# Reading the input without its token factor for the first seven projection blocks of a fused decoder layer

## The reference

```
xn   = h * rsqrt(mean(h*h over channels) + 1e-6) * norm1        # RMSNorm: one factor per token, one per channel
proj = xn @ w_in                                                # q k v z b a c u b(sc) gate_a gate_b
qkv  = silu(causal depthwise conv of 4 taps (q, k, v))          # q, k are L2-normalised per head
beta = sigmoid(b_raw);  g = -exp(a_log) * softplus(a_raw + dt_bias)
o    = chunked gated delta rule(q, k, v, g, beta)               # 8 heads of 128
y_a  = (rms_norm(o) * silu(z)) @ w_dn_out
y_b  = (sc_b * causal depthwise conv of 3 taps (sc_c * sc_u)) @ w_sc_out
h    = h + (sigmoid(gate_a) * y_a + sigmoid(gate_b) * y_b) @ w_o
h    = h + SwiGLU FFN(rms_norm(h));  out = rms_norm(h) without the meta tokens
```

## Time and profile before

| | |
|---|---|
| time, median of 3 runs | 1100.43 us (1100.04 to 1100.97) |
| time of the profiled execution | 1099.78 us |
| its span, first to last instruction | 1097.8 us |
| mean granted TensorE clock | 0.997 |
| busy: PE | 1077.6 us, 98% of the span |
| busy: PEld, DVE, ACT, POOL | 915.6, 339.0, 467.8, 551.3 us |

### The profile page before, as it was taken

One profiled execution on the slowest core, in us unless ns is written; L12 is line 12 of the kernel. 1 busy time (PEld: TensorE's weight loads), 2 busy tenths in 40 slices (PEclk: granted clock), 3 DMA queues, 4 the chain that ended last, 5 costly groups with the idle time before them and its releaser, 6 DMA issues.

```text
span 1097.8 us, 20326 instructions
## 1 busy us (share of the span) xinstructions
PE 1077.6 (98%) x8301; PEld 915.6 (83%) x8301; DVE 339.0 (31%) x595; ACT 467.8 (43%) x1027; POOL 551.3 (50%) x479
## 2 busy tenths in 40 slices
PE   6999999999999999999999999999999999999996
PEld 6999999999999898978788888878888888888884
DVE  6344545454554545351100112222111111200002
ACT  5565656564746564743422233443222233322221
POOL 4363545444453545363544555655555555555551
PEclk9999999999999999999999999999999999999998
DMA  4222212222212122122522322222232223232322
GB/s 180 75 83 69 78 59 70 78 68 76 72 60 87 60 68 79 59 66 71 173 95 80 112 78 96 96 96 96 96 96 87 92 91 96 97 96 96 96 77 77
DMA packets 27788, 95.45 MB, mean 87 GB/s; under 512 B 2984, under 2 KB 3240, under 8 KB 27696
## 3 DMA queue, kind: packets, MB, share of 16 engines
q1 hardware_dynamic: 26496, 91.77, 25.3%
q10 hardware_dynamic: 1200, 2.38, 0.6%
HBM read 92.03 MB, written 2.11 MB: 86 GB/s over the span
## 4 chain that ended last, share of the span: by engine, by line
PE 95%; DVE 2%; issue 1%; POOL 1%; ACT 0%; DMA 0%; DVEq 0%; SPq 0%; POOLq 0%
PE bank L910 94%; DVE qkv L668 0%; DVE h L905 0%; PE bank L981 0%; POOL w_lo L292 0%; DMA h_in<-h_t 0%; DVE qkv L660 0%; DVE cv L668 0%; PE bank L1098 0%; DVE x_lo L672 0%; POOL x_lo L298 0%; PE bank L977 0%; PE bank L976 0%; ACT cbuf L397 0%; DVE h L902 0%
## 5 line engine op out<-in xcount | busy, mean ns | idle before, releaser
L292 POOL TENSOR_TENSOR w_lo<-w_raw,w_hi 128x512 fp32r<-128x512 f32 x324 | 426.1, 1333 | 489.4 <-ACT w_hi L373 489.3
L910 PE MATMUL bank<-x_hi,w_hi 128*128 128x258 f32 (+2 forms) x896 | 248.2, 335 | 5.5 <-DVE x_lo L672 4.5
L373 ACT ACTIVATE w_hi<-w_raw 128x512 fp32r<-128x512 f32 x324 | 190.1, 623 | 107.1 <-PE bank L910 106.7
L910 PE MATMUL bank<-x_hi,w_lo 128*128 128x258 f32 (+2 forms) x896 | 230.6, 316 | 0.0
L910 PE MATMUL bank<-x_lo,w_hi 128*128 128x258 f32 (+2 forms) x896 | 230.1, 315 | 0.0
L910 PE MATMUL bank<-og_hi,w_hi 128*128 128x512 f32 x416 | 164.7, 396 | 0.0
L910 PEld LDWEIGHTS bank<-x_hi,w_hi 128*128 128x128 f32 x896 | 147.0, 189 | 21.0 <-issue 4.3
L910 PE MATMUL bank<-og_hi,w_lo 128*128 128x512 f32 x416 | 164.3, 395 | 0.0
L910 PE MATMUL bank<-og_lo,w_hi 128*128 128x512 f32 x416 | 164.3, 395 | 0.0
L910 PEld LDWEIGHTS bank<-x_hi,w_lo 128*128 128x128 f32 x896 | 147.0, 188 | 11.2
L910 PEld LDWEIGHTS bank<-x_lo,w_hi 128*128 128x128 f32 x896 | 147.5, 189 | 8.6
(11 more groups left out here) (240 smaller groups left out, 1276.6 us busy)
## 6 DMA issues: line engine op xcount, KB each, us to landing
w_raw<-w_stream SPq DMA_DIRECT2D x162, 512.0 KB, 3.3
h_in<-h_t SPq DMA_DIRECT2D x4, 528.0 KB, 5.0
h<-h_t ACTq DMA_DIRECT2D x1, 2048.0 KB, 9.8
out<-h SPq DMA_DIRECT2D x8, 256.0 KB, 2.1
h_in<-gc_dram SPq DMA_DIRECT2D x7, 264.0 KB, 3.2
cst<-consts SPq DMA_DIRECT2D x1, 512.0 KB, 8.0
h_in<-gc_dram ACTq DMA_DIRECT2D x1, 264.0 KB, 3.0
sm<-small SPq DMA_DIRECT2D x1, 80.5 KB, 6.1
```

The costliest lines, as they stand in the source:

```text
L292: nc.gpsimd.tensor_tensor(w_lo[:, n % 2, at], w_raw[:, n % 3, at], w_hi[:, n % 2, at].bitcast(f32), ALU.subtract).then_inc(wlo_ready, 1)
L373: return nc.scalar.activation(to, x, ACT.Copy)
L910: return nc.tensor.matmul(o, w, x, start=start, stop=stop)
```

## The change

The input of head 0's seven blocks is the input times `norm1` alone (`xp_hi`, `xp_lo`), without the token factor; DVE multiplies each of their results by `rs1` as it leaves PSUM. The normalised input `x_hi`, `x_lo` is made in blocks 2 to 6, written in place into `h_in` first, two tiles per block, and is first read by block 7 (`PLAIN`). The token sums move from before block 0 into block 1, behind k = 2. `WARM` goes from 28 + 9 to 16. The high part of weight block 0 moves from ACT to DVE, that of block 1 ahead of ACT's loop. The `small` array (norm1 and others) is loaded first, weight block 0 right behind the first two tiles. The turn of the token projections moves from block 1 to block 2, and ACT's part of `token_factors` to quarter 3 of block 2. Up to block 7, ACT's Silu of q, k, v moves from quarter 0 to quarter 3. `rs1`, the rows of decays and a few other buffers get memory of their own, and `h_in` is protected until its low parts are made.

```diff
-WARM = 28
+WARM = 16
+PLAIN = 7
+XN_AT = {2: (0, 1), 3: (2, 3), 4: (4, 5), 5: (6, 7)}
...
 # SP
+            sp.dma_start(sm[:, :], small[:, :]).then_inc(small_in, 16)
             for part in range(4):
                 sp.dma_start(h_in[:, 2 * part:2 * part + 2, :], h_t[:, 2 * part:2 * part + 2, :]).then_inc(h_loaded[part], 16)
-            sp.dma_start(sm[:, :], small[:, :]).then_inc(small_in, 16)
-            for n in range(STREAM):
+                if part == 0:
+                    sp.dma_start(w_raw[:, 0, :], w_stream[0, :, :]).then_inc(w_in[0], 16)
+            for n in range(1, STREAM):
...
 # POOL
-            for k in range(1, KT, 2):
-                pool.wait_ge(xhi_ready, k + 1)
-                nc.gpsimd.tensor_tensor(x_lo[:, k, :], xnf[k % 4], x_hi[:, k, :].bitcast(f32),
-                                        ALU.subtract).then_inc(xlo_ready, 1)
...
             for n in range(STREAM + 1):
+                for k in XN_AT.get(n - 1, ()):
+                    pool.wait_ge(xhi_ready, k + 1)
+                    nc.gpsimd.tensor_tensor(x_lo[:, k, :], h_in[:, k, :], x_hi[:, k, :].bitcast(f32),
+                                            ALU.subtract).then_inc(xlo_ready, 1)
                 for q in range(4):
...
 # ACT
+            def plain_high(k):
                 act.wait_ge(h_loaded[k // 2], 16)
+                nc.scalar.activation(xp_hi[:, k, :], h_in[:, k, :], ACT.Copy,
+                                     scale=sm[:, NORM1 + k:NORM1 + k + 1]).then_inc(xphi_ready, 1)
+            def square(k):
                 if k >= 4:
                     act.wait_ge(x_added, max(1, k - 4))
-                nc.scalar.activation(xnf[k % 4], h_in[:, k, :], ACT.Square).then_inc(x_squared, 1)
+                nc.scalar.activation(squares[k % 4], h_in[:, k, :], ACT.Square).then_inc(x_squared, 1)
+            act.wait_ge(small_in, 16)
+            plain_high(0)
+            plain_high(1)
+            square(0)
+            square(1)
+            for k in range(2, KT):
+                plain_high(k)
...
-            split_weights(0, 0)
-            split_weights(0, 1)
+            split_weights(1, 0)
+            split_weights(1, 1)
+            for k in range(2, KT):
+                square(k)
+            act.wait_ge(ba_in, 16)
+            copy(wba_hl[:, :, 0:16], wba[:, :].rearrange("p (k c) -> p k c", c=16)).then_inc(wba_hi_ready, 1)
             act.wait_ge(x_sums, 1)
...
-            for k in range(KT):
-                act.wait_ge(xn_ready, k + 1)
-                copy(x_hi[:, k, :], xnf[k % 4]).then_inc(xhi_ready, 1)
...
                         if h < 0 and step == 22:
+                            act.wait_ge(xlo_ready, 1)
                             act.wait_ge(rows_out, 16)
...
-                if kind in ("q", "k", "v"):
+                if kind in ("q", "k", "v") and m:
...
-                if kind == "c":
+                if kind == "c" and m:
...
+                    if m == 0:
+                        act.wait_ge(z_scaled, 1)
+                    nc.scalar.activation(zs[:, m % 2, :], p[0][:, :] if m else zs[:, 0, :], ACT.Silu).then_inc(zs_ready, 1)
...
-                    if q == 0 and 2 <= n and n - 2 < MAIN and BLOCKS[n - 2][0] in ("q", "k", "v"):
+                    if q == 0:
+                        for k in XN_AT.get(n - 1, ()):
+                            act.wait_ge(xn_ready, k + 1)
+                            copy(x_hi[:, k, :], h_in[:, k, :]).then_inc(xhi_ready, 1)
+                    if q == 3 and n == 2:
+                        token_factors()
+                    if q == (0 if n > PLAIN else 3) and 2 <= n and n - 2 < MAIN and BLOCKS[n - 2][0] in ("q", "k", "v"):
                         silu(*BLOCKS[n - 2])
                     if q == 2 and n in EXP_LN_FROM:
                         nc.scalar.preload_act_table_set("natural_log_exp_and_others")
-                if n == 1:
-                    token_factors()
...
 # DVE
+            dve.wait_ge(w_in[0], 16)
+            for half in range(2):
+                at = slice(512 * half, 512 * half + 512)
+                nc.vector.tensor_copy(w_hi[:, 0, at], w_raw[:, 0, at]).then_inc(whi_first, 1)
+            dve.wait_ge(small_in, 16)
+            def plain_low(k):
+                dve.wait_ge(xphi_ready, k + 1)
+                nc.vector.scalar_tensor_tensor(xp_lo[:, k, :], h_in[:, k, :], sm[:, NORM1 + k:NORM1 + k + 1],
+                                               xp_hi[:, k, :].bitcast(f32), ALU.mult, ALU.subtract).then_inc(xplo_ready, 1)
...
+            for k in range(4):
+                plain_low(k)
+            add_square(1)
+            for k in range(4, KT):
+                plain_low(k)
+            for k in range(2, KT):
+                add_square(k)
             link(nc.vector.tensor_scalar(on_scaled[:, :], sm[:, ONORM:ONORM + 1], float(128) ** 0.5, None, ALU.mult))
-            dve.wait_ge(rs1_ready, 1)
...
             dve.wait_ge(wba_hi_ready, 1)
             nc.vector.tensor_tensor(wba_hl[:, :, 16:32], ...).then_inc(wba_ready, 1)
+            dve.wait_ge(rs1_ready, 1)
...
+                    if m == 0:
+                        dve.wait_ge(zeroed, 1)
+                        if kind == "v":
+                            dve.wait_ge(qkv_ready, 1)
+                        dve.wait_ge(rs1_ready, 1)
+                        last = CQKV + 4 * 8 * i + 3
+                        for s, part in enumerate(token_halves(kind)):
+                            ins = mult(raw[:, c % 2, 3 + part.start:3 + part.stop], p[s][:, 0:part.stop - part.start], rs1[:, part])
+                        for s, part in enumerate(token_halves(kind)):
+                            skip = META - TAIL if kind == "q" and s == 0 else 0
+                            at = slice(part.start + skip, part.stop)
+                            ins = nc.vector.scalar_tensor_tensor(cv[:, c % 2, at], p[s][:, skip:part.stop - part.start],
+                                                                 sm[:, last:last + 1], rs1[:, at], ALU.mult, ALU.mult)
+                        ins.then_inc(raw_ready, 1)
...
+                if kind == "z" and m == 0:
+                    mult(zs[:, 0, :], p[0][:, :], rs1[:, META:L]).then_inc(z_scaled, 1)
+                if kind == "c" and m == 0:
+                    for s, part in enumerate(token_halves(kind)):
+                        ins = mult(cbuf[:, part], p[s][:, 0:part.stop - part.start], rs1[:, part])
+                    link(ins)
+                    mult(cbuf[:, TAIL:L], cbuf[:, TAIL:L], rs1[:, TAIL:L]).then_inc(c_ready, 1)
...
-                    mult(ybf, p[0][:, :], cv[:, conv_number("u", m) % 2, META:L]).then_inc(yb_ready, 1)
+                    ins = mult(ybf, p[0][:, :], cv[:, conv_number("u", m) % 2, META:L])
+                    if m == 0:
+                        link(ins)
+                        ins = mult(ybf, ybf, rs1[:, META:L])
+                    ins.then_inc(yb_ready, 1)
...
-                        nc.vector.tensor_copy(bat[:, s * HALF:(s + 1) * HALF], dbank[s][0:32, 0:HALF])
+                        mult(bat[:, s * HALF:(s + 1) * HALF], dbank[s][0:32, 0:HALF], rs1[0:32, s * HALF:(s + 1) * HALF])
...
                 if n == 2:
                     token_decays()
+                for k in XN_AT.get(n, ()):
+                    nc.vector.scalar_tensor_tensor(h_in[:, k, :], h_in[:, k, :], sm[:, NORM1 + k:NORM1 + k + 1], rs1[:, :],
+                                                   ALU.mult, ALU.mult).then_inc(xn_ready, 1)
...
 # PE
-            pe.wait_ge(x_added, KT - 1)
-            for s in range(2):
-                ins = mm(big[0][s][:, 0:HALF], ones, sums1[:, s * HALF:(s + 1) * HALF])
-            ins.then_inc(x_sums, 1)
-            for _ in range(WARM // 3):
-                mm(dbank[3][:, 0:128], ones, ones)
...
                     if n == 0:
-                        pe.wait_ge(xlo_ready if k % 2 else xlo_even, k // 2 + 1)
+                        pe.wait_ge(xplo_ready, k + 1)
+                    if n == PLAIN:
+                        pe.wait_ge(xlo_ready, k + 1)
...
-                    if n == 1 and k == 3:
+                    if n == 1 and k == 2:
+                        pe.wait_ge(x_added, KT - 1)
+                        for s in range(2):
+                            ins = mm(dbank[2 + s][:, 0:HALF], ones, sums1[:, s * HALF:(s + 1) * HALF])
+                        ins.then_inc(x_sums, 1)
+                    if n == 2 and k == 0:
                         turn_token_projections()
```

More of the change, by code:

```diff
@@ L85, in hybrid_block_kernel @@
         eps = sb("eps", [128, 2])
+        plain_mem = ExitStack()
+        xp_hi = sb("xp_hi", [128, KT, L], f32r, plain_mem)
+        plain_mem.close()
         og_hi = sb("og_hi", [128, KT, T], f32r)
@@ L90, in hybrid_block_kernel @@
         x_lo = sb("x_lo", [128, KT, L], f32r, mix_mem)
+        plain_mem = ExitStack()
+        xp_lo = sb("xp_lo", [128, KT, L], f32r, plain_mem)
+        plain_mem.close()
         yb_hi = sb("yb_hi", [128, KT, T], f32r, mix_mem)
```

(48 more changed lines are left out.)

27 lines of the change are left out of this document (12 added, 15 removed).

## The result

The changed kernel takes 1114.74 us (median of 4 runs, 1113.83 to 1114.77) against 1100.43: ratio 1.0133, 95% interval 1.0121 to 1.0145, so 14.3 us slower. The prediction was 1108.7, range 1099 to 1113: the sign was right, the size 6 us short, and the time lies outside the range.

A forecast was written before the change was run, and what follows sets the result against it. PE was taken as the bound from 27.4 us on, so the end moves with block 7's start. Terms from -9.1 to +4.75 summed to +8.95, by clock times +8.5, giving 1108.7 us; range 1099 to 1113.

The forecast's parts named there:

- Front, -9.1: Opening: PE finishes block 0 at 18.3 us, 9.1 earlier than before.
- rival 3: Wait before the token projections: clock falls to 0.5, 1.7 us lost, total 1110.4; chance 0.2.
- q out of PSUM, 0.65: Before block 2: PE waits 0.65 us until DVE has taken q out of PSUM.
- Block 4, 2.1: Before block 4: PE waits 2.1 us for POOL's low part of its weights, queued behind two x_lo.
- Sums of k, 2.7 and 0.5: Behind block 4's tiles: PE waits 2.7 us before the sums of k, then 0.5 for POOL before block 5.
- The v turn, 0.95: Block 5: PE, turning v behind k = 1, waits 0.95 us for Silu of v.
- two loads of 1.28: ACT in block 5: one extra load for Silu of v, one for Ln and Exp at step 24, 1.28 us each.
- PE waits 4.75: Before block 6: PE is done with block 5 at 68.05 and waits 4.75 us for POOL's weight low part.
- Block 6, 8.8 + 0.4: Block 6 takes 8.8 us again, plus 0.4 for two x_lo ahead of block 7's low part.
- Rival 1: DVE's lateness is absorbed before block 3 ends, so only the front's terms stay: 1097.6 us; chance 0.15.
- Rival 2: DVE's taps rarely meet POOL's operations; block 5 starts some 4.5 us earlier, total 1104.5; chance 0.17.
- rival 4: Blocks 6 and 7: DVE and POOL operations meet more often than followed, total above 1113 us; chance 0.05.

The follow-up runs named there:

- e4_late: Changed kernel with the x_hi copies and x_lo subtractions moved behind the split of the next weight block in blocks 3 to 6: 1111.27 us.
- e1_table: Changed kernel with the preload of the Ln and Exp set in block 4 moved behind Silu of v: 1106.2 us, ratio 1.006.
- e2_fill: Changed kernel with 18 products of ones on PE between block 0 and the token projections: 1113.51 us.
- e3_both: Changed kernel with the preload behind Silu of v and 18 products of ones before the token projections: 1104.01 us.
- e11: Changed kernel with the preload behind Silu of v and the making of the normalised input cut to 8 of 528 columns: 1098.77 us, ratio 0.9992.
- e12_resched_nonorm: Changed kernel with token projections behind block 1, preload behind Silu of v, making of the normalised input cut to 8 columns: 1093.06 us, ratio 0.9939.
- e9: Changed kernel with token projections behind block 1, preload behind Silu of v, x parts behind the weight split, and DVE normalising tiles later: 1099.65 us.

## Why the prediction was wrong

The place of the loss, its sign and most of its terms were right. Point by point:

- *Front, -9.1*: 9.2 earlier, with the end at 18.5 for 18.3. Right.
- *Wait of 4.6 before the projections*: 4.0. Right. *Projections 3.9*: **6.3**. This is rival 3, priced at 1.7 with a chance of 0.2; it cost 2.4, and a second and third time further on. The price took 3.5 us at half rate, for which the trace of before has no row (and its clock is 1.00 from the start on, not lower as the rival says); in after PE ran 5.4 us at half rate from 22.50 on.
- *Sums over partitions, +1.15*: from block 1's start to its end 6.9, as forecast (6.95).
- *q out of PSUM, 0.65*: 1.30. The missing part is one small operation with two SBUF inputs, which took 1.20 behind POOL's `w_lo`; I had counted it as "one small". *k, 0.25*: none.
- *Block 4, 2.1*: 0.73. POOL's low part came 1.5 later than forecast (about 52.4 for 50.9), but PE came 3.0 later (51.85 for 48.8), so PE's own delay took the place of the wait. *Sums of k, 2.7 and 0.5*: 2.46 and 0.42. Right.
- *The v turn, 0.95*: no wait. ACT's load of 62.05 is there, but block 5 started 1.5 later than forecast and ran at clock 0.80 (7.79 x 0.20 = 1.6 lost), so PE reached the turn later. In e4_late, where block 5 starts at 59.75, the wait is there: 1.17.
- ***"two loads of 1.28"***, and with it *"PE waits 4.75"*: **the failed step.** There are five additional loads, one for Silu and four for Ln and Exp. The root was forecast done at 67.9 and is done at 72.4; three loads more are 3.8 of these 4.5. Block 6 waits 7.26. My text on the kernel before counts one set for Ln and Exp together; that held for the preloaded set, not for the loads that came by themselves. The price per load was right: 1.28, and the next activation 0.01 to 0.02 after it.
- *Block 6, 8.8 + 0.4*: **11.17**, at clock 0.50 until 82.5.

Together: clock 2.4 + 1.6 + 2.4 = 6.4, block 6's wait 2.5, q 0.65, less what was priced too high (block 4 1.4, v 0.95, the first wait 0.6, k 0.25, block 7 0.4, sums of k 0.3): 5.7 more. Block 7 started 6.6 after its forecast (88.66 for 82.05); the rest is block 0's end 0.2, block 2 0.3, block 3 0.4 and block 4 0.1 longer than forecast. Of this only the first two are large. The 3.9 the other way are no proof of good prices: block 4's and v's came off because PE was late. The loads were shown by e1_table (8.2 in all, their clock included). The clock at the projections was shown by e2_fill and e3_both: 2.4 in its stretch, and 2.2 of it in the time of e3_both. The clock in block 5 was not tested by itself.

As a sum of experiments, each counted from the before beside it: preload misplaced 8.2, normalised input beside the blocks 7.2 (e1 to e11), and what is left is -1.05 (e11): 14.3 in all. Of the front's 9.2 us, 4.0 + 2.4 are lost again in front of and in the projections, 1.15 by the sums and 1.3 at q; e12_resched_nonorm, which has the projections later, keeps 6.8. So the change's idea would be worth 6.8 us here if the normalised input came for nothing, and it costs 6.8 to make it in these blocks. Whether another place for it (behind block 7, with head 1's blocks on the plain input too) would pay stays open; it wasn't tried. Rival 1 (0.15, "the queues catch up") was refuted where it said that it would be decided: PE waited at block 4, for POOL's low part; and even e9 with all edits does not get to 1097.6. Rival 2 (0.17, "turns cost less") was refuted too: three taps alone take 2.38, q's took 3.96 and v's 5.21. The time lies in rival 4's stretch (above 1113, 0.05), but the loads and the clock put it there, not its mechanism.

The forecast also leaned too narrow for a structural reason: rival 3 was kept apart from the forecast, as if it could come once or not at all, while the forecast itself contained a second wait, 4.75, longer than the first. A rival that hangs on a long wait has to be applied to every wait in one's own list, down to the 2.7 before the sums of k: it measured 2.46, and the clock fell behind it too.

## What to carry to other kernels

When an activation moves past another one, write down the order of function sets on ACT for the whole stretch, preloads included, and price one load for every change between Silu, Ln and Exp that is left, not one per set that you think of (Copy and Abs needed none here). Work given to helper engines is not free because they are a third or half busy over the span: in the blocks that it falls in, price its turn in the queue ahead of what TensorE waits for, and test it by shrinking that work to a few columns, which tells at once what it costs. And when your own list of waits has a long one, put the lower clock behind each, with the time to recover.
